# Making the context half of the first attention input inside the first block's down projection instead of inside its embedding gate

## What is computed

```
# end of the first block (latent tokens x, 256 of them)
h = rmsnorm(x, ffn_pre_norm)
f = (silu(h @ w_ffn_gate) * (h @ w_ffn_up)) @ w_ffn_down
x = x + rmsnorm(f, ffn_post_norm)
e = sigmoid(x @ w_ple_gate) * (p @ w_ple_proj)
x = x + rmsnorm(e, ple_post_norm)
# start of the second block (latent tokens x, and 256 context tokens ctx)
xn = rmsnorm(x,   norm_mix) * (1 + sc_m)  + sh_m
xc = rmsnorm(ctx, norm_mix) * (1 + csc_m) + csh_m
y, yc = diff_attention(xn, xc, ...)
```

## Time and profile before

| | us |
|---|---|
| median of 3 runs | 1479.68 |
| lowest and highest | 1477.42, 1482.13 |
| the profiled execution, its own time | 1476.76 |
| its span, first to last instruction | 1474.8 |
| mean granted TensorE clock (share of full) | 0.98 |

### The profile page before, as it was taken

How to read it: one execution, slowest core, us unless ns; L and a number is a source line. 1 busy time by engine, 2 the same in 40 slices (tenths; PEclk the granted TensorE clock), 3 DMA queues, 4 the chain that set the end, 5 groups by cost and what they waited for, 6 DMA issues and landing times.

```text
span 1474.8 us, 25862 instructions
## 1 busy us (share of the span) xinstructions
PE 1413.6 (96%) x9156; PEld 1260.9 (85%) x9156; DVE 711.0 (48%) x1313; ACT 608.8 (41%) x972; POOL 853.9 (58%) x426
## 2 busy tenths in 40 slices
PE   8998999999899999699999999999989999999998
PEld 7998999999887888587788888888878788899997
DVE  5884555556724554735655655343433384311111
ACT  6346544444534444534322323322322265444452
POOL 4785688897545765251443533544364543588895
PEclk8999899999999999999999999999999999999999
DMA  7643477786322222021555565644284101455563
GB/s 292 227 147 122 144 277 275 273 300 211 122 86 72 72 72 86 15 86 47 209 201 190 182 217 177 214 138 175 69 228 121 58 0 59 142 179 185 177 212 101
DMA packets 83194, 227.26 MB, mean 154 GB/s; under 512 B 23872, under 2 KB 29248, under 8 KB 82880
## 3 DMA queue, kind: packets, MB, share of 16 engines
q1 hardware_dynamic: 82688, 224.91, 45.2%
q10 hardware_dynamic: 448, 1.57, 0.4%
HBM read 222.26 MB, written 1.05 MB: 151 GB/s over the span
## 4 chain that ended last, share of the span: by engine, by line
PE 50%; issue 23%; POOL 22%; DVE 2%; ACT 1%; POOLq 0%; SPq 0%; DMA 0%; DVEq 0%; ACTq 0%
POOL wl L521 18%; PE ps L1015 14%; PE ps L1017 14%; PE ps L1016 14%; PE ps L1102 1%; PE ps L1078 1%; PE ps L1079 1%; PE ps L1080 1%; PE ps L1351 1%; PE ps L1277 1%; PE ps L1298 1%; ACT wh L622 1%; PE ps L1365 1%; POOL xl L555 1%; PE ps L1343 1%
## 5 line engine op out<-in xcount | busy, mean ns | idle before, releaser
L521 POOL TENSOR_TENSOR wl<-raw,wh 128x1024 fp32r<-128x1024 f32 x310 | 743.7, 2419 | 544.4 <-ACT wh L622 543.9
L1015 PE MATMUL ps<-xh,wh 128*128 128x256 f32 (+1 forms) x1728 | 564.9, 327 | 22.5 <-POOL wl L521 12.9
L1016 PE MATMUL ps<-xl,wh 128*128 128x256 f32 (+1 forms) x1728 | 557.8, 323 | 0.0
L1017 PE MATMUL ps<-xh,wl 128*128 128x256 f32 (+1 forms) x1728 | 557.5, 323 | 0.0
L622 ACT ACTIVATE wh<-raw 128x1024 fp32r<-128x1024 f32 x310 | 318.5, 1053 | 291.7 <-PE ps L1017 189.2
L1015 PEld LDWEIGHTS ps<-xh,wh 128*128 128x128 f32 x1728 | 332.2, 192 | 59.3 <-POOL wl L521 17.3
L1017 PEld LDWEIGHTS ps<-xh,wl 128*128 128x128 f32 x1728 | 332.6, 192 | 24.5
L1016 PEld LDWEIGHTS ps<-xl,wh 128*128 128x128 f32 x1728 | 332.8, 193 | 22.9
L1015 PE MATMUL ps<-fh,wh 128*128 128x256 f32 (+1 forms) x528 | 168.7, 320 | 1.7 <-POOL wl L521 1.7
L1017 PE MATMUL ps<-fh,wl 128*128 128x256 f32 (+1 forms) x528 | 169.1, 320 | 0.0
L1016 PE MATMUL ps<-fl,wh 128*128 128x256 f32 (+1 forms) x528 | 169.0, 320 | 0.0
(11 more groups left out here) (222 smaller groups left out, 1668.9 us busy)
## 6 DMA issues: line engine op xcount, KB each, us to landing
raw<-wall SPq DMA_DIRECT2D x310, 512.0 KB, 3.7
ada_late<-wada SPq DMA_DIRECT2D x56, 512.0 KB, 3.4
ada<-wada SPq DMA_DIRECT2D x40, 512.0 KB, 3.5
bias<-rpb SPq DMA_DIRECT2D x16, 256.0 KB, 6.4
h<-xin SPq DMA_DIRECT2D x2, 1024.0 KB, 7.3
sww<-qk SPq DMA_DIRECT2D x32, 64.0 KB, 2.0
csb<-cond SPq DMA_DIRECT2D x1, 1024.0 KB, 8.1
sw<-u ACTq DMA_DIRECT2D x2, 512.0 KB, 6.6
```

The costliest lines, as they stand in the source:

```text
L521: nc.gpsimd.tensor_tensor(wl[:, slot, :, :], raw[:, slot, :, :], wh[:, slot, :, :].bitcast(F32), ALU.subtract).then_inc(lo_ready, 1)
L1015: nc.tensor.matmul(o, wa, xa, start=start, stop=False, skip_group_check=True)
L1016: nc.tensor.matmul(o, wa, xb, start=False, stop=False, skip_group_check=True)
L1017: return nc.tensor.matmul(o, wb, xa, start=False, stop=stop, skip_group_check=True)
```

## The change

It moves the context half of the attention input. The modulation of its two parts (0, 1) is done by DVE at the head of its work on the down projection, that of the other parts (3, 4, 2) stays where it was. After the copy of pair 0 DVE scales context tiles 0 to 3; after that of pair 1 it writes the low parts of tiles 0 to 3 and scales 4 to 7; after that of pair 2 it writes the low parts of 4 to 7. ACT writes the high parts of 0 to 3 after the squares of pair 0 and those of 4 to 7 after the squares of pair 1. The scratch has four tiles and lies in the unused right half of `y`. The four transposes move from the norm "fpost1" to "fpre1". POOL and PE wait for other counts of the same semaphores, since the low parts of the context now come ahead of those of the gate's input.

```diff
-CTX_TILES = (range(0, 3), range(3, 6), range(6, KT))
+CTX_TILES = (range(0, 4), range(4, KT))
@@ POOL
-            input_lows(h, 3 * KT)
+            input_lows(h, 4 * KT)
@@ ACT, stream_summed, after square_pair
+                        if name == "fpost1" and j < 3 * ph.per_pair:
+                            split_part(2 * KT, 0, 1, CTX_TILES[j // ph.per_pair - 1], y[:, 0:4, SEQ:NT], 4)
@@ ACT, embedding gate, after the sigmoid
-                if p < 3:
-                    split_part(2 * KT, 0, 1, CTX_TILES[p], yc)
@@ PE, norm_sum
-                    for t in range(4 if name == "fpost1" else n // P):
+                    for t in range(4 if name == "fpre1" else n // P):
@@ PE
-            features(PH["pg"], SEQ, fresh=("xl_ready", 3 * KT, 1))
+            features(PH["pg"], SEQ, fresh=("xl_ready", 4 * KT, 1))
@@ DVE, take_summed, after the copy of pair p
+                    if norm == "fpost1":
+                        lows = CTX_TILES[p - 1] if 1 <= p < 3 else ()
+                        scaled = CTX_TILES[p] if p < 2 else ()
+                        modulate_part(0, 1, (), lows, y[:, 0:4, SEQ:NT], 4)
+                        if scaled and lows:
+                            dve.wait_ge(S("xl_ready"), 3 * KT + len(lows))
+                        modulate_part(0, 1, scaled, (), y[:, 0:4, SEQ:NT], 4)
@@ DVE
+            modulation(0, (0, 1), 1)
             take_summed(PH["dn"], y, "fpost1")
             recip("fpost1", SEQ)
             add_normed(y, par_ap("ffn_post"))
...
-            modulation(0, (0, 1, 3, 4, 2))
+            modulation(0, (3, 4, 2), 2)
             for p in range(4):
...
-                modulate_part(0, 1, CTX_TILES[p] if p < 3 else (), CTX_TILES[p - 1] if p else (), yc)
```

More of the change, by code:

```diff
@@ L208, in build @@
         sq = at("sq", [P, KT, NT], xs_at)
-        yc = at("yc", [P, KT, SEQ], big_at)
         fh = {SEQ: at("fh1", [P, FT, SEQ], big_at, F32R), NT: at("fh2", [P, FT, NT], big_at, F32R)}
@@ L724, in split_shifted, with split_part @@
                                              bias=mod[:, l, section(l, shift) + k, c:c + 1]).then_inc(S("xh_ready"), 1)
-            def split_part(count0, l, c, tiles, src):
+            def split_part(count0, l, c, tiles, src, slots=KT):
                 for k in tiles:
                     act.wait_ge(S("xr_ready"), count0 + k + 1)
-                    nc.scalar.activation(xh[:, k, c * SEQ:c * SEQ + SEQ], src[:, k, :], ACT.Identity,
+                    nc.scalar.activation(xh[:, k, c * SEQ:c * SEQ + SEQ], src[:, k % slots, :], ACT.Identity,
                                          bias=mod[:, l, section(l, 0) + k, c:c + 1]).then_inc(S("xh_ready"), 1)
@@ L1472, in modulate, with modulate_part @@
                 lagged(scaled, low, 2)
-            def modulate_part(l, c, tiles, lows, to):
+            def modulate_part(l, c, tiles, lows, to, slots=KT):
                 t = slice(c * SEQ, c * SEQ + SEQ)
@@ L1479, in modulate_part @@
                     for k in tiles[n_:n_ + 1]:
-                        V.scalar_tensor_tensor(to[:, k, :], h[:, k, t], gsc[:, l, 0, k, c:c + 1], rstd_ps[:, t],
+                        V.scalar_tensor_tensor(to[:, k % slots, :], h[:, k, t], gsc[:, l, 0, k, c:c + 1], rstd_ps[:, t],
                                                ALU.mult, ALU.mult).then_inc(S("xr_ready"), 1)
@@ L1486, in modulate_part @@
                         dve.wait_ge(S("xh_ready"), xh_count[0])
-                        V.scalar_tensor_tensor(xl[:, k, t], to[:, k, :], mod[:, l, section(l, 0) + k, c:c + 1],
+                        V.scalar_tensor_tensor(xl[:, k, t], to[:, k % slots, :], mod[:, l, section(l, 0) + k, c:c + 1],
                                                xh[:, k, t].bitcast(F32), ALU.add, ALU.subtract).then_inc(S("xl_ready"), 1)
@@ L1513, in condition, with modulation @@
                     ins.then_inc(ada_used, 1)
-            def modulation(l, parts):
+            def modulation(l, parts, gains):
                 last_row = l * ADA_UNITS + max(section(l, part) for part in parts) + KT
@@ L1530, in modulation @@
                                                ALU.add, ALU.mult).then_inc(S("gsc_ready"), 1)
-                dve.wait_ge(S("gsc_ready"), 2 * (l + 1))
+                dve.wait_ge(S("gsc_ready"), gains)
             def low_tile(src, n, k):
@@ L1748, in _ @@
                 if l:
-                    modulation(1, range(6))
+                    modulation(1, range(6), 4)
                 recip(f"m{l}", NT if l else SEQ)
@@ L1910, in _ @@
                 if l == 0:
-                    modulation(0, (5,))
+                    modulation(0, (5,), 2)
                 take_gated(PH[f"dn{l}"], n, l, 1, ("m1", "final")[l])
```

## The result

The changed kernel takes 1485.84 us (median of 6 runs, 1482.51 to 1487.29) against 1479.86 for the kernel before (6 runs on the same chip, 1475.75 to 1482.13): a ratio of 1.0041, 95% interval 1.0023 to 1.0059. It is slower by some 6 us, a little over what a measurement here can tell. The profiled execution of the changed kernel took 1486.91 us, with a span of 1485.0. Most lines of the changed kernel have other numbers by one than before: the low parts L1487 are now L1486, the scalings L1480 are L1479, the copy L1599 is L1598, the sigmoid L872 is L873.

The account below looks back on a forecast made before the run. PE, busy 96%, was taken as bound by its waits, chiefly a gate stall from ACT's in-order queue. Terms -4.7 + 7.1 + 2.2 = +4.6 us, added to 1479.68, gave 1484.3; range 1476 to 1489, the forecast's own 1481 to 1488.

Parts of the forecast that it names:

- The gate, -4.7: Embedding gate: removing context work saves 4.7 us, made of 2.4 and 0.5 waiting and 1.7 low clock.
- Rival C: Embedding gate: its gain doesn't come, POOL or a weight load being late next; 1489 us, chance 0.09.
- The down projection, +7.1: Down projection: added DVE and ACT work makes DVE late for PE's norm, costing 7.1 us, PE's stalls included.
- a slip of 0.5: Down projection, pair 0: ACT's next high part comes later and POOL slips some 0.5 us, covered by PE's lead.
- 1.4 was forecast: Down projection, pair 1: PE stalls some 1.4 us for POOL's low part, and 0.4 two units on.
- 8.7 (347.2 to 355.9): Down projection, pair 2: four low parts pass at POOL's changes of unit, 348.2 and three times 2.55 later.
- the end of pair 2's copy: Down projection: DVE's copy ends at 347.2 instead of 344.03, after a load landing 3.7 later, high part and squares.
- The clock, +2.2: Norm behind the down projection: PE's idle stretch brings a low clock, costing 2.2 us, bounds 1.6 to 2.8 doubled.
- Transposes, 0: Two transposes move from one norm to another, both on the path: zero, give or take 0.3 us.
- A: Down projection: low parts cost only what they last, 0.40 us; net -4.7 to -2.9, 1475.0 to 1476.8; chance 0.15.
- B: Down projection: one or two fewer low parts blocked; net -1 to +2, 1479 to 1482 us; chance 0.16.
- The point from which the low parts decide the sign: Down projection, pair 2: from three blocked low parts downwards the loss is under the gate's gain.

Follow-up runs that it names:

- e6: Kernel before, with only ACT's order in the gate changed: high parts of next weight units ahead of the context tiles; 1483.18 us, ratio 1.0028.
- e8: The changed kernel run again without edit, on the second chip, giving its second profile; 1487.81 us, ratio 1.0064.
- e1: Changed kernel, but low parts of context tiles 4 to 7 written in the embedding gate instead of behind pair 2's copy; 1476.23 us, ratio 0.998.
- e2: Changed kernel, but the four low parts behind pair 2 subtract a PSUM tensor, leaving out the true low parts; 1477.96 us, ratio 0.9983.
- e5: Changed kernel with e1's low parts in the gate and e3's second scratch together; 1473.63 us, ratio 0.9972.
- e7: Changed kernel with two of pair 2's four low parts (tiles 6 and 7) moved into the gate; 1478.0 us, ratio 1.0006.
- e3: Changed kernel with a second four-tile scratch: behind pair 1 DVE scales 4 to 7, then writes low parts 0 to 3 without waiting; 1483.45 us, ratio 1.0024.

## Why the prediction was right

The mechanism that was forecast is the one that happened, and its sign: 1485.84 against 1484.3, inside the forecast's own range of 1481 to 1488. Step by step, in the order of its terms:

**The gate, -4.7.** Measured -4.6 (17.8 against 22.4 us from first to last sigmoid), with ACT's high parts directly behind the sigmoid and no wait of PE over 0.3 us for weights. Rival C falls. What the prediction did not see is that the queue order on ACT was only part of the cause: by its text (weight preparation "stands behind context work that nobody needs yet"), reordering should have been enough, and e6 shows that it isn't.

**The down projection, +7.1.** Measured +10.3. The same stretch in the second profile gives +9.3. Pair 0 cost PE nothing; POOL idled 1.68 us there (0.53 in e8) where a slip of 0.5 was forecast. In pair 1 one low part was held and three passed: 2.99 us for four, ACT's wait 4.26, PE's stall 2.1 where 1.4 was forecast (1.1 to 1.6 in the five other profiles with this chain). In pair 2 all four were held: 9.16 us where 8.7 (347.2 to 355.9) was forecast. Then 8.5 us of conditioning and squares (360.34 to 368.81), as forecast. The mis-sized term is the end of pair 2's copy. It was forecast for 347.2 and came at 351.33; less the 1.25 us by which this profile reached the down projection later, that is 2.9 us late. The step was: the last unit's load "lands 3.7 later". That is the median over all 310 loads of the kernel. The load in question was issued at 342.66 and landed 6.3 us later, and ACT waited 3.19 us for it. Loads issued in pairs 1 and 2 of the kernel before had also taken 5.5 to 6.6 us, with the DMA engines 93% busy over 326 to 343; ACT had waited at most 2.6 us for one of them. 2.6 us of the 2.9 are this, the rest is the load's issue, 0.4 later than forecast. About 1 us of the 2.9 is scatter of this one profile: by the same reckoning the copy is 1.9 us late in e8, where ACT waited 3.55 us for that load. SP's wait of 5.2 us for conditioning work, which looks like the culprit in its list of waits, is not: it ended at 338.7, ahead of the weight loads at 340.30 and 342.66, which went out as POOL freed their places.

**The clock, +2.2.** Measured 2.1 against before, and 2.3 against kernels of the same form without the idle stretch (16.1 against 13.9 in e1, e2 and e5). The clock was low for longer (0.52 and 0.50 through 363 to 377) than behind the gate's stall, but PE had no work until 368.9.

**Transposes, 0.** From first sums to first sigmoid, e1 and e5 take 13.9 us against 14.1 before, with two transposes fewer; within the bounds given.

**The rivals.** A (low parts at what they last) was true for three of four in pair 1 and for none in pair 2; e2 made it true there and gave 1477.96, 2.4 under its kernel before, where A was given 2.9 to 4.7 under; an interval of 3 us each way holds both. B (fewer held) is e7: 0.4 us under its own kernel before, inside the -1 to +2 given for it. Its 1478.0 lies under the 1479 to 1482 that was made of this with the first chip's time. The point from which the low parts decide the sign, forecast as three held (a line that left out the clock: 4.6 of delay against 4.7 of gain), is nearer to two: two held gave 96.5 us in the stretches against 96.7 before, four gave 104.4, so three would by interpolation already be a loss of some 4. Three were not tried.

The sum of the stretches is +7.8 and +6.8 in two profiles where the prediction had +4.6. That 1484.3 comes so near to 1485.84 is in part luck: the medians of the two comparisons say +6.0 and +9.5, and the terms were 2 to 3 us short.

## What to carry to other kernels

Before moving work into DVE's idle time, look at what POOL does in that time: here an instruction of 0.4 us with two SBUF inputs took up to one POOL instruction (2.1 to 2.6 us in the mean of a group) beside a POOL that is back to back, and its own 0.4 in a gap of 2 us, or with one operand in PSUM. Removing a gap of POOL therefore had a price on DVE, and an order that shortened one wait moved it to the next norm; count DVE's two-SBUF instructions on both sides of an edit. For a load on the path take the landing time from the stretch where it is issued, not the page's median.

## What was unexpected of the hardware

- POOL hardly pays for what DVE pays: with four DVE low parts held among them its units take 12.50 / 5 = 2.50 us, against 11.76 / 5 = 2.35 just before them, 0.7 us for four intrusions, while DVE lost 7.5.
- The size of the held instruction made no difference here: 128x16 operations (L1527) take 2.3 us each beside POOL in e6 (4.69 for two), as much as 128x256 low parts (2.26).
- A gap of 1.91 us on POOL was enough for four low parts to pass at 0.4 each (e3).
- An idle stretch of 2.5 us ahead of the norm cost 0.3 us through the clock, one of 3.7 (e3) and one of 8.0 cost 2.3 each. 80 fillers gave the 2.3 back in this stretch, though the median shows only 0.7 of it.
